# Four moved steps, and scores ahead of sums in the paired attentions

## The reference

```
# ahead of each layer: h = rmsnorm(x, g) * (1 + scale) + shift, with shift, scale, gate = split(silu(c) @ w_ada + b_ada)
# layer 1: z = h @ ev_w_in ; MLA attention (8 heads) and sliding-window attention (8 heads, window 128, sink)
cq  = rmsnorm(z_cq, q_norm)      # 384 channels, 3 rows of 128
ckv = rmsnorm(z_ckv, kv_norm)    # 256 channels, 2 rows of 128
o = concat(o_mla, o_swa) * silu(z_gate);  y = o @ w_out
# layer 2: differential attention (4 heads of 128) and forgetting attention (8 heads of 64)
o_d = rmsnorm(o_d, subln) * (1 - lam_init)      # the "head norm"
o = concat(o_d, o_f) * silu(z_gate);  y = o @ w_out
# layer 3: conformer convolution (width 31), then a squared-ReLU MLP (4096 wide)
# layer 4: gated recurrence, 8 heads, forwards and backwards, then an MLP
o = o * rsqrt(mean(o * o, -1) + eps) * gn_g * silu(g)     # each head of the recurrence
```

## Time and profile before

| | us |
|---|---|
| median of three executions | 2214.53 (2212.08 to 2215.33) |
| profiled execution | 2211.57, its span 2209.8 |
| PE busy | 2090.9 (95% of the span) |
| DVE busy | 1460.2 (66%) |
| ACT busy | 916.0 (41%) |

### The profile page before, as it was taken

How to read it: one execution, slowest core, us unless ns; L and a number is a source line. 1 busy time by engine, 2 the same in 40 slices (tenths; PEclk the granted TensorE clock), 3 DMA queues, 4 the chain that set the end, 5 groups by cost and what they waited for, 6 DMA issues and landing times.

```text
span 2209.8 us, 26686 instructions
## 1 busy us (share of the span) xinstructions
PE 2090.9 (95%) x9920; PEld 1614.1 (73%) x9920; DVE 1460.2 (66%) x2641; ACT 916.0 (41%) x1737; POOL 16.3 (1%) x15
## 2 busy tenths in 40 slices
PE   4888999999998999999999999999999989999998
PEld 2665567777666776677888887788888777888886
DVE  6577775767365599977565555899989865333333
ACT  3344553344443342344232233666565644232231
POOL 1000000000000000000000000000000000000000
PEclk8999999999898899999999999999999999999999
DMA  8422322433223211134555552211111112232231
GB/s 330 172 98 71 92 72 72 136 141 117 93 94 101 73 58 57 39 118 145 186 190 176 194 177 81 67 48 58 58 49 58 48 58 77 87 106 95 95 96 58
DMA packets 65983, 228.75 MB, mean 104 GB/s; under 512 B 7104, under 2 KB 9280, under 8 KB 65728
## 3 DMA queue, kind: packets, MB, share of 16 engines
q1 hardware_dynamic: 65856, 227.05, 30.9%
HBM read 224.93 MB, written 2.10 MB: 103 GB/s over the span
## 4 chain that ended last, share of the span: by engine, by line
PE 72%; DVE 18%; ACT 6%; issue 4%; DMA 1%; DVEq 0%; SPq 0%; ACTq 0%
PE bank L377 19%; PE bank L379 19%; PE bank L378 19%; DVE arena L1737 6%; PE bank L2023 3%; PE bank L649 2%; DVE w_lo L315 2%; PE bank L683 1%; PE bank L1188 1%; PE bank L1213 1%; DVE arena L497 1%; ACT arena L1231 1%; DVE arena L1969 1%; PE bank L1202 1%; ACT w_hi L306 1%
## 5 line engine op out<-in xcount | busy, mean ns | idle before, releaser
L377 PE MATMUL bank<-h_hi,w_hi 128*128 128x512 f32 (+1 forms) x1616 | 665.6, 412 | 22.6 <-DVE h_lo L643 14.6
L379 PE MATMUL bank<-h_hi,w_lo 128*128 128x512 f32 (+1 forms) x1616 | 638.1, 395 | 0.0
L378 PE MATMUL bank<-h_lo,w_hi 128*128 128x512 f32 (+1 forms) x1616 | 636.3, 394 | 0.0
L306 ACT ACTIVATE w_hi<-w_raw 128x1024 fp32r<-128x1024 f32 (+3 forms) x293 | 290.9, 994 | 294.9 <-PE bank L379 282.7
L315 DVE TENSOR_TENSOR w_lo<-w_raw,w_hi 128x1024 fp32r<-128x1024 f32 (+3 forms) x290 | 333.2, 1151 | 88.9 <-ACT w_hi L306 88.5
L377 PEld LDWEIGHTS bank<-h_hi,w_hi 128*128 128x128 f32 (+1 forms) x1616 | 307.4, 190 | 98.4 <-issue 30.2
L379 PEld LDWEIGHTS bank<-h_hi,w_lo 128*128 128x128 f32 (+1 forms) x1616 | 306.2, 189 | 68.2
L378 PEld LDWEIGHTS bank<-h_lo,w_hi 128*128 128x128 f32 (+1 forms) x1616 | 307.4, 190 | 61.2 <-issue 4.4
L377 PE MATMUL bank<-a_hi_t,w_hi 128*128 128x512 f32 x512 | 203.0, 396 | 0.0
L378 PE MATMUL bank<-a_lo_t,w_hi 128*128 128x512 f32 x512 | 203.0, 396 | 0.0
L379 PE MATMUL bank<-a_hi_t,w_lo 128*128 128x512 f32 x512 | 202.9, 396 | 0.0
(11 more groups left out here) (258 smaller groups left out, 2448.4 us busy)
## 6 DMA issues: line engine op xcount, KB each, us to landing
w_raw<-weights_dram SPq DMA_DIRECT2D x261, 512.0 KB, 3.6
ada_raw<-ada_dram SPq DMA_DIRECT2D x128, 512.0 KB, 3.6
arena<-ada_dram SPq DMA_DIRECT2D x8, 1024.0 KB, 15.7
w_raw<-weights_dram SPq DMA_DIRECT2D x16, 256.0 KB, 2.6
xT<-x_dram SPq DMA_DIRECT2D x1, 2048.0 KB, 14.5
out_dram<-xT SPq DMA_DIRECT2D x8, 256.0 KB, 2.2
tables<-tables_dram SPq DMA_DIRECT2D x1, 1536.0 KB, 19.8
w_raw<-weights_dram SPq DMA_DIRECT2D x8, 144.0 KB, 3.4
```

The lines of the kernel that those rows point to most:

```text
L306: nc.scalar.activation(WH[:, slot, 0:w], RAW[:, raw, 0:w], ACT.Copy).then_inc(w_hi_ready, 1)
L377: nc.tensor.matmul(o, WH[:, slot, cols], self.hi(k), start=(k == 0), stop=False)
L378: nc.tensor.matmul(o, WH[:, slot, cols], self.lo(k), start=False, stop=False)
L379: last = nc.tensor.matmul(o, WL[:, slot, cols], self.hi(k), start=False, stop=(k == self.K - 1))
```

## The change

1. The opening's reciprocal step (step 8 of `n1`) moves from 4.5 to 5.3 in the order, behind one more `FirstAda` step, and `first_hi` and `first_lo` with it; the later steps of `n1` follow in other groups. `Norm.dve_step` no longer waits for its `ready` marks (x, or the rows of `a1`) at step 0; the wait for the root, in step n, stays.
2. `nq` and `nk` get `lag=1`: the PE takes a row's sum of squares one step later.
3. `HeadNorm` takes each sum one step later too.
4. `yp` takes its chunks in the order 4, 5, 6, 0, 1, 2, 3, 7, each with a wait of its own, and no wait for all of `hn`.
5. In the recurrence `scale_dve` moves from level 3 to level 4, behind the evacuation and the part of the woven projection.
6. In `PairAttention.pe_step` the scores of unit u go ahead of the sums of unit u - 2.

```diff
--- before.py
+++ after.py
@@ -352,7 +352,8 @@
         class Project(Stage):
 
 
-            def __init__(self, count, K, M, hi, lo, ready, evac, evac_engine="act", dve_work=None, chunks=None, ada=None, banks=(0, 1, 2, 3), parts=1, outer=1):
+            def __init__(self, count, K, M, hi, lo, ready, evac, evac_engine="act", dve_work=None, chunks=None, ada=None, banks=(0, 1, 2, 3), parts=1, outer=1, order=None):
+                self.order = order or range(K)
                 self.ada, self.parts, self.outer = ada or {}, parts, outer
                 self.steps = count * parts + (1 if parts > 1 else 0) - (outer - 1)
                 self.n0, self.count, self.K, self.M = next_tile[0], count, K, M
@@ -372,11 +373,12 @@
 
             def matmuls(self, t, ks):
                 slot, o = (self.n0 + t) % RING, bank[self.banks[t]][0:self.M, :]
-                for k in ks:
+                for i in ks:
+                    k = self.order[i]
                     cols = slice(k * self.M, (k + 1) * self.M)
-                    nc.tensor.matmul(o, WH[:, slot, cols], self.hi(k), start=(k == 0), stop=False)
+                    nc.tensor.matmul(o, WH[:, slot, cols], self.hi(k), start=(i == 0), stop=False)
                     nc.tensor.matmul(o, WH[:, slot, cols], self.lo(k), start=False, stop=False)
-                    last = nc.tensor.matmul(o, WL[:, slot, cols], self.hi(k), start=False, stop=(k == self.K - 1))
+                    last = nc.tensor.matmul(o, WL[:, slot, cols], self.hi(k), start=False, stop=(i == self.K - 1))
                 return last
 
             def place_of(self, i):
@@ -409,10 +411,11 @@
                 if p == 0:
                     pe.wait_ge(*lower_half(self.n0 + t))
                     free_bank(pe, self.before[t])
-                for k in range(p * self.K // self.parts, (p + 1) * self.K // self.parts):
+                for i in range(p * self.K // self.parts, (p + 1) * self.K // self.parts):
+                    k = self.order[i]
                     if self.chunks and t == 0 and self.chunks[k]:
                         pe.wait_ge(self.chunks[k].sem, self.chunks[k].at(1))
-                    last = self.matmuls(t, (k,))
+                    last = self.matmuls(t, (i,))
                 if p == self.parts - 1:
                     last.then_inc(tile_done, 1)
 
@@ -532,7 +535,8 @@
         class Norm(Stage):
 
 
-            def __init__(self, src, n, gain, bias, hi, lo, at, scratch_kb=16, ready=(), out=None, add=None, func=None, layer=False, sums=4, scratch=None):
+            def __init__(self, src, n, gain, bias, hi, lo, at, scratch_kb=16, ready=(), out=None, add=None, func=None, layer=False, sums=4, scratch=None, lag=0):
+                self.lag = lag
                 self.src = src if callable(src) else lambda k: src[:, k, :]
                 self.n, self.gain, self.bias, self.hi, self.lo, self.at = n, gain, bias, hi, lo, at
                 self.sq, self.t, self.h, self.rstd, self.mean = scratch or norm_scratch(scratch_kb)
@@ -558,7 +562,8 @@
                         free_bank(pe, self.before_mean)
                         for c in range(self.n):
                             nc.tensor.matmul(bank[6][:], ones, self.src(c), start=(c == 0), stop=(c == self.n - 1)).then_inc(self.sq_used.sem, 1)
-                if k < self.n:
+                k -= self.lag
+                if 0 <= k < self.n:
                     pe.wait_ge(self.sq_ready.sem, self.sq_ready.at(k + 1))
                     nc.tensor.matmul(self.bank[:], ones, self.sq[:, k % 2, :], start=(k == 0), stop=(k == self.n - 1)).then_inc(self.sq_used.sem, 1)
 
@@ -599,8 +604,6 @@
 
             def dve_step(self, dve, i):
                 if i == 0:
-                    for m, c in self.ready:
-                        dve.wait_ge(m.sem, m.at(c))
                     if self.layer:
                         dve.wait_ge(self.mean_ready.sem, self.mean_ready.at(1))
                         for k in range(self.n):
@@ -1166,10 +1169,10 @@
                         pe.wait_ge(m.sem, m.at(k))
                     for b in (4, 5, 6, 7):
                         free_bank(pe, self.before[b])
+                if s % 2 == 0 and u < U:
+                    self.pe_scores(pe, u)
                 if s % 2 == 0 and 2 <= u < U + 2:
                     self.pe_sums(pe, u - 2)
-                if s % 2 == 0 and u < U:
-                    self.pe_scores(pe, u)
                 if 1 <= u < U + 1:
                     self.pe_turn(pe, u - 1, s % 2)
 
@@ -1398,17 +1401,17 @@
         def even_layer():
             n1 = Norm(XT, C, lambda k: GAIN[:, k:k + 1], lambda k: MOD[:, k:k + 1], HH, HL, 0,
                       scratch=(view(72, (2, S)), view(76, (2, S)), None, view(80, (S,)), None), ready=[(x_here, 16), (ones_here, 16)])
-            weave((n1, -1, 0.1, 0, C), (FirstAda(), 0, 1), (n1, 4.5, 1, C, C + 1), (Do(act=first_hi, pool=first_lo), 4.55, 1), (n1, 4.6, 0.15, C + 1, C + 3),
-                  (n1, 5.3, 0.3, C + 3, C + 5), (n1, 6.3, 0.3, C + 5, C + 7), (n1, 7.3, 0.3, C + 7, 2 * C + 2))
+            weave((n1, -1, 0.1, 0, C), (FirstAda(), 0, 1), (n1, 5.3, 1, C, C + 1), (Do(act=first_hi, pool=first_lo), 5.35, 1), (n1, 5.4, 0.15, C + 1, C + 4),
+                  (n1, 6.3, 0.3, C + 4, C + 6), (n1, 7.3, 0.3, C + 6, 2 * C + 2))
             G, Q, KV, Z = view(0, (8, S)), view(16, (8, S)), view(32, (8, S)), view(48, (12, S))
             VM, VS, tmp = view(72, (NT, 8, 64)), view(80, (NT, P)), view(82, (S,))
             KR, SK, SV, SQ = 5, 6, 7, 8
 
             a1 = Project(12, C, P, HH, HL, [], plain_evac(Z, 0), chunks=n1.split, ada=ada_next(range(12)), outer=3)
             nq = Norm(Z[:, 0:3, :], 3, lambda k: vec("q_norm", k), None, HH, HL, 0, scratch=(view(16, (2, S)), view(20, (2, S)), None, view(28, (S,)), None),
-                      ready=[(a1.free, 3)], sums=6)
+                      ready=[(a1.free, 3)], sums=6, lag=1)
             nk = Norm(Z[:, 3:5, :], 2, lambda k: vec("kv_norm", k), None, HH, HL, 4, scratch=(view(24, (2, S)), view(72, (2, S)), None, view(30, (S,)), None),
-                      ready=[(after(a1.free, 3), 2)], sums=7)
+                      ready=[(after(a1.free, 3), 2)], sums=7, lag=1)
             tv = Tokens([(Z[:, SV, :], 0, P, VS, after(a1.free, SV))], banks=(6,))
             whole = slice(0, P)
             r2 = Rope([(Z[:, z, :], whole, after(a1.free, z)) for z in (SK, SQ, SQ + 1, SQ + 2, SQ + 3)], "perm64", "cos64", "sin64", view(44, (S,)), view(46, (S,)))
@@ -1478,10 +1481,11 @@
                 n = self.n
                 if i == 0:
                     free_bank(pe, self.before)
-                if i < n:
-                    pe.wait_ge(self.squared.sem, self.squared.at(i + 1))
+                if 1 <= i <= n:
+                    k = i - 1
+                    pe.wait_ge(self.squared.sem, self.squared.at(k + 1))
                     for j in range(NT):
-                        last = nc.tensor.matmul(self.bank[:, NT * i + j:NT * i + j + 1], self.sq[i % 2][:, j * P:(j + 1) * P], ones[:, 0:1], start=True, stop=True)
+                        last = nc.tensor.matmul(self.bank[:, NT * k + j:NT * k + j + 1], self.sq[k % 2][:, j * P:(j + 1) * P], ones[:, 0:1], start=True, stop=True)
                     last.then_inc(self.summed.sem, 1)
                 elif n < i <= 2 * n:
                     k = i - n - 1
@@ -1614,7 +1618,8 @@
             Y = view(50, (8, S))
             oh = lambda k: HH[:, k, :] if k < 4 else FH[:, k - 4, :]
             ol = lambda k: HL[:, k, :] if k < 4 else FL[:, k - 4, :]
-            yp = Project(8, C, P, oh, ol, [(hn.split, 4)], plain_evac(Y, 0), chunks=[None] * 4 + [after(fox_out.done, k) for k in range(4)], ada=ada_next(range(7)))
+            yp = Project(8, C, P, oh, ol, [], plain_evac(Y, 0), chunks=[after(m, k) for m in (hn.split, fox_out.done) for k in range(4)],
+                         ada=ada_next(range(7)), order=(4, 5, 6, 0, 1, 2, 3, 7))
             post = TokenNorm(Y, C, lambda k: GAIN[:, 8 + k:9 + k], yp.free, added=7, out=lambda k: XT[:, k, :], add=lambda k: XT[:, k, :], busy=(7, (2, 1, 3)))
             post_gain = gate_gain(1)
             pre, pre_gain = second_norm(0, 0, post.normed, banks=(5,), busy=(7, (1, 1, 2)))
@@ -2252,13 +2257,13 @@
                     if l == 2:
                         H.key_decay(dve, u + 1)
                         H.query_decay(dve, u + 1)
-                    if h and l == 3:
+                    if woven and l == 4:
+                        woven.evacuate(dve, 0)
+                        woven.dve_part(dve, 0)
+                    if h and l == 4:
                         H.scale_dve(dve, h - 1)
                     if h and l == 5:
                         H.gate_out(dve, h - 1)
-                    if woven and l == 4:
-                        woven.evacuate(dve, 0)
-                        woven.dve_part(dve, 0)
                     if woven and l == 6:
                         woven.evacuate(dve, 1)
```

## The result

The changed kernel takes 2191.34 us (median of 4, 2190.52 to 2193.17); the kernel before took 2213.31 in the same comparison (4 runs, 2208.57 to 2215.33). The ratio is 0.9892, 95% interval 0.9876 to 0.9909: 24 us less (20 to 27), against 24.0 forecast and a forecast time of 2190.5 (the two medians differ by 22.0). The sum came out within two microseconds, but one of its seven terms had the wrong sign, and the clock and three terms that gave more than forecast made up for most of it. That part is luck, and it is what the rest is about.

The account below looks back on a forecast made before the run. TensorE, with matmul work in 95% of 2209.8 us, sets the end, so only its 119 us idle and its clock can give. Seven terms sum to -24.0 us, from a median of 2214.5 to 2190.5; range 2177 to 2204.

Parts of the forecast that it names:

- Opening: Before the first projection: a later reciprocal, chunk 0 about 1 us later, two PE stops become one; -1 us, bounds -2.8 and +2.
- Latent norms: Five PE stops before the sums of squares go when each sum comes one tile later; -7.6 us, bounds -8.4 and -4.
- rival 2: Stops only change place: DVE and ACT take back gains in norms and head norm, ACT holds the recurrence; 2204 us, chance 0.13.
- Attentions: In 48 paired-attention units, scores fill PE stops at the sums and come earlier at the ends; -3.9 us, bounds -12 and +10.
- the other stops stand at the turns, and the swap leaves them: In the paired attentions, PE stops between a unit's copy and turn stay unchanged when scores go ahead of sums; no gain counted.
- Head norm: Three PE stops for ACT's square go, 3.9 us, less 1 for ACT's root waiting on the fourth sum; -2.9 us.
- Output projection: The PE's 2.91 us wait for the head norm's fourth split goes whole by taking ready chunks first; -2.9, bounds -3.3 and -2.
- Recurrence: With the scale later, DVE no longer waits for ACT's root, ending a 0.63 us PE stop in six heads; -3.8 us.
- its next stop is 17 us later: In the recurrence, DVE's 2.21 us wait for the root is carried on to its next stop, at 1484.11.
- the PE stop of 0.63 gone six times: Expected sign in the recurrence's trace: the PE's 0.63 us stop disappears in each of six woven heads.
- Clock: With stops of 2.05 and 2.91 us gone, part of the forgetting-attention stretch may stay at 2.4 GHz; -1.9, bounds 0 and -9.
- The lower level follows stops: Stretches at 1.2 GHz come after PE stops; in the forgetting-attention stretch about 10 us of matmul time runs at half speed.

Follow-up runs that it names:

- Swap alone: Kernel before with only the scores of unit u put ahead of the sums of unit u-2 in the attentions: ratio 0.9957.
- the kernel with the query's product later: Kernel before with only DVE's product of the next head's query and its sigmoid moved from level 1 to level 2 of the recurrence: ratio 1.0006.

## Why the prediction was right, and where it was not

- **Opening**: forecast -1, in the trace -1.8, by the steps foretold (29.0, 3.36, reciprocal later, one stop for two).
- **Latent norms**: -7.6, in the trace -8.1 at the first scores. Five stops, one late last sum, nothing of DVE's tail in the way: rival 2 did not happen here.
- **Attentions**: -3.9. Swap alone: 1.6 and 0.6 in layer 1, 2.1 at the end, clock included; about right in sum. A detail was wrong: "the other stops stand at the turns, and the swap leaves them"; at the end it shortens them by 1.6 us. Where a unit's whole chain is what the PE waits for, earlier scores bring all of it forward.
- **Head norm**: forecast -2.9, and 3.9 of stops went. ACT's wait at the root for the fourth sum holds up nobody on the PE; the 1 us set aside for it was not paid.
- **Output projection**: -2.9 forecast, -3.1 by ratio, no stop in the trace.
- **Recurrence**: forecast -3.8, measured +3.6, shown in two kernels. This is the step that failed: "behind the evacuation and w_lo of step 4 the root is long there" is true, but "its next stop is 17 us later" is not. DVE's next stop was 3 us later, in a row of the kernel before that the prediction passed over:

```profile
1469.49 1.23 DVE L315 TENSOR_TENSOR w_lo<-w_raw,w_hi 128x1024 fp32r<-128x1024 f32 x1 [0.20 <-ACT w_hi L306]
```

A wait of only 0.20 us, but on ACT: it sets `w_lo`'s start whatever DVE did before, so DVE's 2.21 us were never carried on to 1484.11, and the scale was hidden ahead of it. The prediction's sign, "the PE stop of 0.63 gone six times", did not come: it stands six times at 0.61 or 0.62, and six new ones of 0.49 with it. Rival 2 said that the later stop is held by ACT's chain; that fits every trace here but was not tried by itself.
- **Clock**: forecast -1.9, about -5. A gain of the head norm's stretch (0.81 to 0.94), of `yp`'s and the attention's, less losses in layer 1's norms and the convolution. "The lower level follows stops" holds for the head norm by the executions above, and not everywhere (last section).

So -24.0 was -22.1 of stops and -1.9 of clock; in the trace it is -16 and -5. With the recurrence's sign put right the forecast's stops would have been -22.1 + 3.8 + 3.6 = -14.7. The total was right by luck: an error of 7.4 us one way met several the other way, 3.1 of clock, 1.0 of the head norm, 0.8 of the opening, 0.5 of the norms, 5.4 in all. The spans differ by 21.1 us, the medians by 22.0, the ratio says 23.9: that lies within what executions of one kernel differ (below).

Do the parts add up? The single edits' ratios, without the recurrence's, come to 1.7%, 38 us, while the kernel with all five gained 1.2%, 26 us (21 to 31). The granted clock, known for every execution, settles it. Take (1 - mean clock) x time out of each execution's time and average over all executions of a kernel, each against the kernel before on the same chip:

| kernel | clock part | rest |
|---|---|---|
| norms' lag alone | -3.7 | -7.1 |
| opening alone | -0.6 | -1.5 |
| head norm alone | -8.4 | -2.6 |
| swap alone | -3.5 | -4.7 |
| `yp` order alone | -1.1 | -1.7 |
| sum of the five | -17.2 | -17.6 |
| all but the recurrence edit | -7.8 | -18.2 |
| recurrence edit alone | +0.9 | +2.7 |

The rest adds up: 17.6 against 18.2 us, with some 2 us of scatter, and the prediction's five terms for these edits come to 18.3. The clock's part does not add up: each edit alone got clock back, 17.2 us in sum, and all together 7.8. Why the five together get no more stays open, and so does which execution gets which stretches at 1.2 GHz.

## What to carry to other kernels

Before moving work out of a stop, look for the engine's next wait on another engine, however short: work ahead of it may have been free, and behind it is on the path. An engine that keeps a stop of the same length wherever an instruction is moved is waiting for its supplier; move the supplier's queue (here ACT's root, which took the PE's new stop away), not the consumer. Don't add up edits measured one by one without looking at the clock of each execution. And cut both traces at the same instructions and read the clock column of each piece before giving an edit credit.

## What was not expected of the hardware

One kernel's time follows the clock that it is granted, by executions: the kernel with the query's product later ran on one chip in 2208.40 and 2208.65 us at a mean clock of 0.976 and in 2219.85 and 2221.16 at 0.970. 0.006 x 2210 = 13 us, and the times differ by 11 to 13. A stretch at 1.2 GHz needs no stop of the PE right before it either: the changed kernel's layer 1 norms ran at 0.87 with the PE busy 64.99 of 67.00 us. The clock was at 1.00 from 350 to 358 us, with the PE busy all 8.00 us, and at 0.53 from 358 to 376; the last stop before was one of 1.60 us at 347.98. What made it fall there no run shows.
